# Two mixture-of-experts layers on one core: expert blocks of 32 tokens instead of 64, in four column tiles

## The reference

```python
def first_block(x, ...):            # rms norm, attention + LRU + conformer branches, w_out, then
    h2 = rms_norm(x, norm2_g[l]).reshape(bsz * seq, d)
    x = x + hierarchical_moe(h2, router_coarse[l], router_fine[l], exp_w_gate[l], exp_w_up[l], exp_w_down[l])

def trunk_layer(x, ctx, c, c_ctx, ...):   # the second block
    # context path: 256 context tokens through the same mixer, from which only two states s_fwd, s_bwd are kept
    hx = modulate(rmsnorm(x, norm1_g), mod_x[0], mod_x[1])
    ...                                     # Fourier mix and a bidirectional gated delta rule that starts from the states
    x = x + mod_x[2] * mixer_output(...)
    x = x + mod_x[5] * moe_ffn(modulate(rmsnorm(x, norm2_g), mod_x[3], mod_x[4]), ...)
# final: rmsnorm(x, final_g)

# either expert layer: one of 4 groups by top-1, two of its 8 experts by top-2, for each of 512 tokens
#   y[token] += gate * ((silu(x @ w_gate[e]) * (x @ w_up[e])) @ w_down[e])
#   w_gate, w_up: 1024 x 512, w_down: 512 x 1024, 32 experts; 1024 token-expert pairs a layer
```

## Time and profile before

| | us |
|---|---|
| median of 3 runs | 1801.9 |
| the profiled execution | 1797.79 |
| its span | 1796.0 |
| PE busy | 1673.9 (93%) |
| DVE busy | 657.9 (37%) |
| ACT busy | 444.3 (25%) |
| POOL busy | 170.5 (9%) |
| first layer's first matmul of weights | at 352.31 |
| second layer's | at 1276.06 |

### The profile page before, as it was taken

The page is one execution under the profiler, slowest core; times in us unless marked ns, Lnnn a source line. Parts: engine busy times, 40 slices in busy tenths (PEclk is TensorE's granted clock), DMA queues, the critical chain, the costliest instruction groups (busy, mean ns, idle before and its releaser), DMA issues.

```text
span 1796.0 us, 21821 instructions
## 1 busy us (share of the span) xinstructions
PE 1673.9 (93%) x8694; PEld 857.8 (48%) x8694; DVE 657.9 (37%) x1266; ACT 444.3 (25%) x803; POOL 170.5 (9%) x172
## 2 busy tenths in 40 slices
PE   7999999799999999999699997999799999999993
PEld 3455454445445555455345557965433333333331
DVE  3279341432222212122469937542522222221213
ACT  2233771133221112111348412232000000000001
POOL 0000000011111111110000013100111111111100
PEclk9999999799999999999899998999799999999987
DMA  9265531499999999999470191055899999999995
GB/s 366 101 241 182 189 141 47 152 399 402 393 408 405 406 405 399 403 413 410 175 270 1 13 137 48 1 227 216 318 394 396 404 410 399 409 419 411 423 421 214
DMA packets 95324, 519.45 MB, mean 289 GB/s; under 512 B 22509, under 2 KB 28237, under 8 KB 70648
## 3 DMA queue, kind: packets, MB, share of 16 engines
q1 hardware_dynamic: 84024, 500.66, 72.0%
q0 software_dynamic: 11200, 17.39, 2.9%
HBM read 508.19 MB, written 29.15 MB: 299 GB/s over the span
## 4 chain that ended last, share of the span: by engine, by line
PE 69%; DMA 14%; issue 8%; DVE 5%; ACT 2%; SPq 2%; DVEq 0%; POOLq 0%
PE bank L868 22%; PE bank L884 11%; PE bank L461 8%; PE bank L469 7%; DMA ring<-in_w_up 6%; PE bank L825 3%; PE bank L855 3%; DMA ring<-in_w_down 2%; DMA arena<-in_w_down 2%; PE bank L895 2%; PE bank L527 2%; PE bank L692 2%; PE bank L454 1%; DVE arena L2643 1%; DMA ring<-diag 1%
## 5 line engine op out<-in xcount | busy, mean ns | idle before, releaser
L870 PE MATMUL bank<-ring,arena 128*64 128x512 f32 x912 | 413.2, 607 | 0.0
L868 PE MATMUL bank<-ring,arena 128*64 128x512 f32 x896 | 402.9, 603 | 7.9 <-DMA ring<-in_w_up 4.6
L2542 DVE TENSOR_TENSOR arena<-arena,bank 64x512 f32<-64x512 f32 x70 | 48.3, 690 | 557.5 <-ACT arena L1837 557.5
L461 PE MATMUL bank<-arena,ring 128*128 128x512 f32 x560 | 244.6, 593 | 0.0
L868 PEld LDWEIGHTS bank<-ring,arena 128*64 128x64 f32 x896 | 119.7, 139 | 243.3 <-issue 236.7
L884 PE MATMUL bank<-ring,arena 128*64 128x512 f32 x424 | 193.2, 598 | 2.0 <-DMA ring<-in_w_down 2.0
L886 PE MATMUL bank<-ring,arena 128*64 128x512 f32 x424 | 193.2, 598 | 0.0
L1476 POOL DMA_INDIRECT arena<-xnd,smalli x70 | 67.8, 969 | 1051.1 <-PE bank L855 535.3
L1837 ACT ACTIVATE arena<-bank 64x512 f32<-64x512 f32 x70 | 41.3, 590 | 509.9 <-PE bank L870 509.9
L461 PEld LDWEIGHTS bank<-arena,ring 128*128 128x128 f32 x560 | 105.2, 190 | 127.0 <-issue 127.0
L870 PEld LDWEIGHTS bank<-ring,arena 128*64 128x64 f32 x912 | 122.5, 139 | 0.0
(11 more groups left out here) (452 smaller groups left out, 2104.8 us busy)
## 6 DMA issues: line engine op xcount, KB each, us to landing
ring<-in_w_up SPq DMA_DIRECT2D x53, 2048.0 KB, 20.6
ring<-in_w_gate SPq DMA_DIRECT2D x52, 2048.0 KB, 17.6
ring<-in_w_down SPq DMA_DIRECT2D x50, 2048.0 KB, 20.0
arena<-in_w_down SPq DMA_DIRECT2D x14, 2048.0 KB, 36.4
ring<-in_w_mod SPq DMA_DIRECT2D x12, 2048.0 KB, 15.5
arena<-in_w_gate SPq DMA_DIRECT2D x12, 2048.0 KB, 34.6
arena<-in_w_up SPq DMA_DIRECT2D x11, 2048.0 KB, 27.4
ring<-in_w_in SPq DMA_DIRECT2D x10, 2048.0 KB, 17.4
```

The source lines that it names most:

```text
L461: mm = pe.matmul(b[:, 0:n], w[:, k, col:col + P], ap[:, k, :], start=(k == 0), stop=(k == KD - 1))
L868: pe.matmul(GU[0:CAP, :], x, wg_[:, c, :], start=(c == 0), stop=(c == KD - 1), skip_group_check=True)
L870: mm = pe.matmul(GU[CAP:2 * CAP, :], x, wu_[:, c, :], start=(c == 0), stop=(c == KD - 1), skip_group_check=True)
```

## The change

Blocks hold 32 tokens. `SIZES` gives each place in the order of experts a number of blocks, 52 in layer 0 and 56 in layer 1, and both layers now take all experts but the first three in order of their counts. A matmul of `gate_up` or `down` has 32 columns of stationary operand and 256 of moving operand, and four of them fill the four column strips of the array: w_gate's two halves and w_up's two halves, or w_down's four quarters.

Rows are gathered and scattered for four blocks at once (128 rows), in whole rows of 4 KB. The rows of the first four blocks aren't gathered: `first_x(e)` multiplies the normed tokens, which are still in `xn_tok`, by one-hot matrices `in_soon` for 64 slots of expert e, 32 matmuls for each of two experts. The second, `first_x(1)`, stands behind `gate_up(0)` on PE. SP's wait for the first gather is replaced by a wait for `first_x(1)` ("first01", "first11"), ahead of wvc in layer 0 and of the weight load 9 in layer 1.

The 64 context steps are dealt over the experts by an even share of an assumed time (6.2 us a block, 2.1 us a step), at up to four places in a block, so that an expert with one block takes more of them. w_down's rows are dealt to partitions in two halves, so a partition's part of a load is two pieces of 8 KB instead of one of 16 KB. The token's weight is no longer applied when Y is emptied, which takes four instructions of 32 x 256, but at the end of layer 1 in place of the plain adds. An extra block now holds 128 tokens and NOV is 31, so the loops have 31 iterations on DVE and ACT and 16 with two `If`s elsewhere.

```diff
-CAP = 64
-NOV = 2 * T // CAP - 1
+CAP = 32
+QUAD = P // CAP
 FIXED = 3
+SIZES = [[2, 2, 2, 1, 1] + [2, 2, 1] * 8 + [2, 1, 1],
+         [2, 2, 2, 1, 1, 1] + [3, 1, 4, 1, 3, 1, 3, 1, 3, 1] + [2, 2, 1] * 4 + [2, 2, 1, 1]]
+NOV = 31
+CONTEXT_STEPS = 64
+PLACES = [[(0, "after"), (0, "down"), (0, "turn"), (0, "half")],
+          [(1, "half"), (0, "down"), (1, "down"), (0, "turn"), (0, "after"), (1, "after")]]
+BLOCK_US, STEP_US = 6.2, 2.1
...
+                def first_x(e):
+                    b = CV.deal(pe, f"first{m}{e}")
...
                     for c in range(KD):
-                        mm = pe.transpose(XT[:, CAP * c:CAP * c + CAP], xg[u][:, c::KD], M["ident"][0:CAP, 0:CAP])
+                        for t in range(TT):
+                            mm = pe.matmul(b[:, 2 * CAP * c:2 * CAP * c + 2 * CAP], xn_tok[:, t, c::KD], in_soon[:, TT * e + t, :],
+                                           start=(t == 0), stop=(t == TT - 1), skip_group_check=True)
...
                     for c in range(KD):
-                        x = xTs[u][:, CAP * c:CAP * c + CAP]
-                        pe.matmul(GU[0:CAP, :], x, wg_[:, c, :], start=(c == 0), stop=(c == KD - 1),
-                                  skip_group_check=True)
-                        mm = pe.matmul(GU[CAP:2 * CAP, :], x, wu_[:, c, :], start=(c == 0), stop=(c == KD - 1),
-                                       skip_group_check=True)
+                        if c == KD // 2 and beside_now(n, "half"):
+                            next(beside, None)
+                        x = xTs[q % 2][:, P * c + CAP * b:P * c + CAP * b + CAP]
+                        for i, (w, col) in enumerate(((wg_, 0), (wg_, 256), (wu_, 0), (wu_, 256))):
+                            mm = pe.matmul(GU[CAP * i:CAP * i + CAP, 0:256], x, w[:, c, col:col + 256],
+                                           start=(c == 0), stop=(c == KD - 1), skip_group_check=True)
...
                 for n in range(last + 1):
                     gate_up(n)
                     if n == 0:
-                        slots()
-                    if n >= ALONE:
+                        first_x(1)
+                    if n == 1:
+                        spots()
+                    if beside_now(n, "after"):
                         next(beside, None)
...
-                sp.wait_ge(S("gathered1"), 16 * (BASE[m] // 2 + 1))
                 if m == 0:
...
                     sp.wait_ge(S("xn_out"), 16 * TT)
+                    sp.wait_ge(CV.full, CV.at("first01"))
                     sp.dma_start(wvc, cols(a["w_in_2"], 3)).then_inc(S("ctx_w"), 16)
                 if m:
-                    sp.wait_ge(S("xn_out"), 16 * TT * 2)
+                    sp.wait_ge(S("x2_out"), 16 * (1 + TT))
                     load_e(1, 8)
...
                     if m and i == 3 * FIXED:
-                        sp.wait_ge(S("x2_out"), 16 * (1 + TT))
+                        sp.wait_ge(S("xn_out"), 16 * TT * 2)
+                        sp.wait_ge(CV.full, CV.at("first11"))
...
+            def split_down(w):
+                return w.rearrange("e (h p c) n -> e p h c n", h=2, c=2)
...
                 def take_y(n):
...
-                    A(ys[q], Y[:, :], ACT.Copy).then_inc(S("y_taken"), 1)
+                    for i in range(4):
+                        ins = A(ys[q % 2][CAP * b:CAP * b + CAP, 256 * i:256 * i + 256], Y[CAP * i:CAP * i + CAP, 0:256],
+                                ACT.Copy)
+                    ins.then_inc(S("y_taken"), 1)
...
-                chain(TTo(o, o, yg[t][0], ALU.add))
-                TTo(o, o, yg[t][1], ALU.add).then_inc(S("x4_ready"), 1)
+                chain(STT(o, yg[t][0], w12[:, t:t + 1], o, ALU.mult, ALU.add))
+                STT(o, yg[t][1], w12[:, TT + t:TT + t + 1], o, ALU.mult, ALU.add).then_inc(S("x4_ready"), 1)
```

More of the change, by code:

```diff
@@ L1010, in moe @@
[L1010 to L1020 removed]
+                b = V.deal(pe, f"order{m}")
@@ L1488, in scatter @@
                         .then_inc(S(f"stored{u}"), 16)
-                for n in range(NB[m] + 2):
-                    if n == 2:
-                        pool.wait_ge(CV.free, CV.at(f"slots{m}"))
-                    if n < NB[m]:
-                        gather(n)
-                    if n == 4:
-                        pool.wait_ge(CV.free, CV.at(f"spots{m}"))
-                    if n >= 4:
-                        scatter(n - 4)
+                pool.wait_ge(CV.free, CV.at(f"slots{m}"))
+                gather(1)
@@ L1500, in experts @@
+                gather(2)
+                pool.wait_ge(CV.free, CV.at(f"spots{m}"))
+                for q in range(3, NQ[m]):
+                    scatter(q - 3)
+                    gather(q)
+                scatter(NQ[m] - 3)
                 baton = S(f"beyond{m}")
@@ new lines, in take_y, with first_x @@
+                    for i in range(4):
+                        ins = TTo(ys[q % 2][CAP * b:CAP * b + CAP, 256 * i:256 * i + 256], Y[CAP * i:CAP * i + CAP, 0:256],
+                                  m5[CAP * i:CAP * i + CAP, :], ALU.mult)
+                    ins.then_inc(S("y_taken"), 1)
+                def first_x(e):
+                    b = take(f"first{m}{e}", CV)
+                    o, o3 = chunks(xTs[0], P)[:, :, 2 * CAP * e:2 * CAP * e + 2 * CAP], [P, KD, 2 * CAP]
+                    ins = TTo(o, chunks(b[:, :], 2 * CAP), bc(gain, 2, o3), ALU.mult)
+                    ins.then_inc(CV.free, 1)
+                    if shift is not None:
+                        own(f"first{m}{e}", CV)
+                        ins = TTo(o, o, bc(shift, 2, o3), ALU.add)
+                        ins.then_inc(S("xs_ready"), 1)
+                    else:
+                        own(f"first{m}{e}", CV)
+                        dve.sem_inc(S("xs_ready"), 1)
@@ new lines, in experts @@
+                dve.wait_ge(S("ranked"), m + 1)
+                dve.sem_inc(V.free, 1)
+                dve.wait_ge(S("gains"), 1 + 2 * m)
+                first_x(0)
+                b = take(f"homes{m}")
+                CP(bc_row, b[:, 0:2 * NE])
+                chain(CP(ordt, b[0:1, 2 * NE:3 * NE]))
+                dve.sem_inc(S("ordered"), 1)
+                dve.sem_inc(V.free, 1)
+                home, cap, many = bc_row[:, 0:NE], bc_row[:, NE:2 * NE], key[:, 0:NE]
+                chain(TTo(many, cnt, cap, ALU.subtract))
@@ L2478, in experts @@
+                o3 = [P, NE, OVER]
+                chain(TTo(over, bc(many, 2, o3), bc(pcol("slot0", 0, OVER), 1, o3), ALU.is_gt))
                 chain(dve.tensor_reduce(nov, over, AX, ALU.add))
```

550 lines of the change are left out of this document (271 added, 279 removed).

## The result

The change made the kernel slower: 1878.9 us median of 4 runs (1875.3 to 1882.2) against 1801.8 (1799.5 to 1804.7), ratio 1.0427 with a 95% interval of 1.0397 to 1.0456. The forecast was 1806 in 1781 to 1831: its side was right, its size was not. The span of the profiled execution went from 1796.0 to 1880.0 us.

What follows compares the result with a forecast made beforehand. The weight DMA stream was taken as the bound, hiding almost all of PE's saving. Layer 0's terms gave -4 us and layer 1's +8, +4 on the 1796.0 span, 1806 us on the median's scale, range 1781 to 1831.

Steps and rivals of the forecast that it cites:

- layer 0's stream: Layer 0's weight loads: PE no longer holds the queue shallow, rate up 1.3% from 404 GB/s, -6 us.
- layer 0's start: First expert of layer 0: one-hot products of 7.3 us each free buffers later, near 372 us; +9 us, bounds 3 and 14.
- both starts: Later loads at the layers' starts: +9 us in layer 0, +4 us in layer 1 (bounds 0 and 10).
- the loops and tails: Layer ends: 31-iteration skipped loops take 16 to 17 us on DVE, 13 to 14 on ACT; +3.4 and +7 us.
- Blocks: PE's expert blocks: quads at 0.216 us each, 6.4 us a block in all, so PE gets slack in both layers.
- rival 3: Expert blocks: four strips don't run together, or PE sits at 1.2 GHz throughout layer 1; +210 us, 2016; 6%.
- rival 4: Extra blocks run because blocks are smaller, each costing its weights in a row, over 30 us; 2%.
- the gain of 7.4 us: End of layer 0: PE finishes at 865 instead of 872.4 us, -7.4 us.
- The sentence on the clock: Layer 1's one-block experts: weight waits drop the clock, 34 us lost from 109 of slack; no term, except up to 1.5.
- Layer 1's stream: Layer 1's weight loads: queue already deep, so 0 for the rate.
- Rival 1: Both layers' streams get faster with a deep queue: at most -18 and -17 us, 1771; half of it 1788; 26%.
- Rival 2: One-block experts: context steps in close succession wait for DVE or ACT; at 6 us of stall each, +24 us, 1830; 12%.

Runs made afterwards that it cites:

- places: Changed kernel with the same 64 context steps at other places in TensorE's order in layer 0; 1841.0 us, ratio 1.0225 to the kernel before.
- gather0: Changed kernel with the first four blocks' rows fetched by one POOL gather instead of the two one-hot products; 1850.3 us, ratio 1.0267 to the kernel before.
- split32: Changed kernel with each 128-row gather issued as four indirect DMAs of 32 rows, fetching other rows for some blocks; 1977.5 us, one extra block included.
- best1: Changed kernel with first rows gathered, context steps moved as in places, and extra-block loops behind one branch; 1803.6 us, ratio 1.0009 to the kernel before.
- best2: best1 with the 2.6 us product for the later rows' indices moved behind the second block's gate/up product; 1799.2 us, ratio 0.9996 to the kernel before.

## Why the prediction was wrong

Two steps failed. The first is layer 0's stream: the term of -6 us, with its premise that PE "gets slack in both" layers, where places shows 37.9 us of loss by the order of PE's work. The second is layer 0's start: two products priced at 7.3 us each took 15.5, and gather0 gives back 28.7 us where the sum had +9 and +4 for both starts. The side, slower, was right by the loops and tails, which are 14 of the 84 us. It didn't foresee the rest, so a sum of +4 us that had the right sign is mostly luck.

1. **Blocks** held. The gate/up products of a block take 3.66 us for 16 quads, 0.229 each (0.216 forecast), and a block 6.2 us (6.4). PE's saving was real, and 32-column strips do run four at a time; rival 3 is out. No extra block ran; rival 4 is out for these inputs; the one extra block that split32 ran cost 63 us ("over 30" forecast).
2. **Layer 0's start failed by size.** The term was two products of 7.3 us "at full clock". They took 15.5 each. The price of a record came from a product (L794 of the earlier trace rows) whose stationary operand lies in one piece; that of `first_x` takes every eighth element of a row (`c::KD`), and its records are 0.238 us apart at both levels of the clock. So the clock, which was at its 1.2 GHz level for most of the stretch, isn't the reason. The stride alone isn't shown to be it either: the transposes of L895 read their stationary operand with the same stride and take 0.71 us for four, but they have one record each and not two. No run separates these. The freeing was forecast for 372 us and came at 399. The 27 us are 6.4 of a later landmark, some 16 of the two products, 6.4 of the clock in the products beside them, less about 2 elsewhere. gather0 gives 18.2 us in layer 0 and 14.0 in layer 1 for the products, against +9 and +4 in the sum for all of the start. The upper bound of 14 was too low for the same reason.
3. **Layer 0's stream was the step that failed in kind.** The prediction compared totals, 479 us of PE against 508 of DMA, and concluded that PE "gets slack in both" and "will no longer hold the queue shallow". Slack in the sum doesn't feed a ring of six buffers. A queue can hold three loads, 15 us; a two-block expert with context steps keeps its buffers for longer than that: from a landed w_down to the next free buffer it took 15.5 us (746.0 to 761.5). The term was -6; of the +53.3 of layer 0 the products account for 18.2 and the places of the steps for 37.5, and with both out (best1) layer 0 takes 533.5 us, 532.7 before. What stays open there is why the gain of 7.4 us that the sum had never came. Also PE is at 1.2 GHz for its next products after 11 of the 13 waits (L930 took 3.45 us at 746.0 and 1.91 at 753.3), which lengthens the hold. The sentence on the clock had this for layer 1, where the DMA share stays at 1.01 in spite of PE's waits, and not for layer 0.
4. **The loops and tails** held: 16.98 us before DVE's L2219 (the counterpart of L2175), 12.73 before the table load, 15.46 before the final adds (16 to 17, 13 to 14, 16), +7.0 at the end. Between the layers it was +7.1 instead of +3.4, of which some 3 us can be the scatter of single executions.
5. **Layer 1's stream:** 0 was taken; it rose from 413 to 422 GB/s, 2.2% of some 490 us, by this estimate about -11. Rival 1 was right here for a cause that it didn't name, the number of indirect DMAs. It can be what holds layer 1 to +10.7 in spite of its start; with the products gone (gather0) layer 1 is 3.3 us shorter than before, so not all of the estimate is seen.
6. **Rival 2** had the right place (context steps beside experts) with the wrong mechanism. PE's waits for DVE or ACT at context lines are under 8 us in all of layer 0; what the steps did was to hold buffers.

What stays open: why best2, with a layer 1 stream of 423 GB/s, gains so little there. Its layer 0 takes 528.7 us from landmark to PE's end (532.7 before) and its layer 1 503.6 (504.7), and the first loads still go out 26.3 us after the landmark in layer 0, 22.2 before. One-block experts first could free them sooner; that wasn't tried. Nor was it tried why the records of the one-hot product are 0.238 us apart, whether the rate depends on whole or half rows scattered; and no run took the share of the low clock in layer 0's loss apart from the waits that cause it.

## What to carry to other kernels

When both engine and DMA are full, don't compare their totals: follow one buffer from the landing of the load that the engine waits for to the next free slot, and hold that time against the loads that are queued behind it. Work put into an in-order stream is free only where the engine would wait anyway, and the same step a few instructions later can cost its full length and more. And a product that replaces a gather is priced from a row that reads its operands in the same way, not from one that only has the same shape, and by who can't get a buffer until it ends.

## What the runs showed of the hardware

Two products with 128-column float32 weights can differ by a factor of two in pace at full clock, and the slower one doesn't notice the clock. L885's records are 0.238 us apart at a granted clock of 1.00 and of 0.50; L954's are 0.112 us apart at 1.00, and those of L946, which has the same form, 0.213 at 0.50. The record of L885's weight loads is nearly as long as the product:

```profile
374.29 15.31 PEld L885 LDWEIGHTS bank<-arena 128*128 128x128 f32 x64 [0.41 <-issue]
```

TensorE can be busy by every record and still be put to its 1.2 GHz level. The second product of layer 0 began at full clock (1.00 in 374.3 to 376 us) and was at 0.50 from 378 us to its end, with PE busy for all of the time:

```profile
374.00:390.00 16.00, 16.00 (x74) 15.60 (x66) 3.49 (x7) 0.38 (x1) 0.00 (x0) 0.60 0.01 1
```

The Trainium skill (TensorE: Matmul & The Clock Gate, Part 1: The HAM clock gate) says that activity releases the throttle and calls the fast state "busy"; by this trace the clock can fall while a product's records fill the time. Its section on HAM oscillation, cited in the prediction for layer 1, describes what layer 0 did: bursts between DMA waits that start throttled, here after 11 of 13 waits.

An indirect DMA has a price in the stream of plain loads that its rows don't explain: at 1.01 share, 17 POOL issues in 300 us went with 422 GB/s and 41 (split32, the same number of rows) with 408.
